# Prompt attention on one core: outputs one unit later in TensorE's order, with second buffers for the transposed weights

## The reference

```python
s_c = einsum(q, kc) * scale + bias ; p_c = masked_softmax(s_c) ; o_c = p_c @ vc
s_s = einsum(q, k_sel) * scale + bias ; p_s = masked_softmax(s_s) ; o_s = p_s @ v_sel
s_w = einsum(q, kw) * scale + bias ; p_w = masked_softmax(s_w) ; o_w = p_w @ vw
o = g[..., 0:1] * o_c + g[..., 1:2] * o_s + g[..., 2:3] * o_w
```

## Time and profile before

| | |
|---|---|
| median of three runs | 1896.12 us |
| profiled execution | 1892.59 us |
| its span | 1890.8 us |
| mean granted clock of TensorE | 0.954 |
| TensorE matmul busy | 1770.0 us, 94% |
| VectorE busy | 836.6 us, 44% |
| ScalarE busy | 525.2 us, 28% |
| prompt attention, first scores to last weighted sum | 201.7 to 329.2 us |

### The profile page before, as it was taken

How to read it: one execution, slowest core, us unless ns; L and a number is a source line. 1 busy time by engine, 2 the same in 40 slices (tenths; PEclk the granted TensorE clock), 3 DMA queues, 4 the chain that set the end, 5 groups by cost and what they waited for, 6 DMA issues and landing times. The chain is left out here.

```text
span 1890.8 us, 36210 instructions
## 1 busy us (share of the span) xinstructions
PE 1770.0 (94%) x15772; PEld 1690.7 (89%) x15772; DVE 836.6 (44%) x1654; ACT 525.2 (28%) x896; POOL 696.1 (37%) x278
## 2 busy tenths in 40 slices
PE   6989798779768999899999999999999999999997
PEld 6987688569745998799999999999999999999997
DVE  4251586225573444465430355444235555024531
ACT  5132454322241222232221222331223222112221
POOL 1300000012202111355653555655655655445641
PEclk8988699989978999899999999999999999999999
DMA  5540420513200100122222222322222222222222
GB/s 146 122 57 23 148 90 13 162 48 94 60 1 22 37 4 28 46 89 90 68 73 85 88 90 65 92 91 90 68 89 90 68 90 73 84 90 90 66 78 76
DMA packets 158379, 140.90 MB, mean 75 GB/s; under 512 B 16178, under 2 KB 153942, under 8 KB 157838
## 3 DMA queue, kind: packets, MB, share of 16 engines
q1 hardware_dynamic: 158222, 138.60, 24.8%
HBM read 132.68 MB, written 10.02 MB: 75 GB/s over the span
## 5 line engine op out<-in xcount | busy, mean ns | idle before, releaser
L270 POOL TENSOR_TENSOR w_lo<-w_raw,w_hi 128x2048 fp32r<-128x2048 f32 (+3 forms) x109 | 459.3, 4214 | 783.9 <-ACT w_hi L264 783.7
L309 PE MATMUL ps<-h_hi,w_hi 128*128 128x288 f32 x2016 | 434.1, 296 | 0.0
L309 PE MATMUL ps<-h_hi,w_lo 128*128 128x288 f32 x2016 | 433.4, 296 | 0.0
L309 PE MATMUL ps<-h_lo,w_hi 128*128 128x288 f32 x2016 | 433.2, 296 | 0.0
L264 ACT ACTIVATE w_hi<-w_raw 128x2048 fp32r<-128x2048 f32 (+3 forms) x109 | 190.1, 1744 | 501.9 <-PE ps L309 458.5
L309 PEld LDWEIGHTS ps<-h_hi,w_hi 128*128 128x128 f32 x2016 | 324.0, 189 | 0.3
L309 PEld LDWEIGHTS ps<-h_hi,w_lo 128*128 128x128 f32 x2016 | 323.7, 189 | 0.0
L309 PEld LDWEIGHTS ps<-h_lo,w_hi 128*128 128x128 f32 x2016 | 323.5, 189 | 0.0
L418 DVE TENSOR_TENSOR xT<-ps,xT 128x576 f32<-128x576 f32 x48 | 35.6, 756 | 264.7 <-PE ps L309 264.7
L309 PE MATMUL ps<-g_lo,w_hi 128*128 128x288 f32 x704 | 151.1, 295 | 0.0
L309 PE MATMUL ps<-g_hi,w_lo 128*128 128x288 f32 x704 | 151.0, 295 | 0.0
(11 more groups left out here) (497 smaller groups left out, 2794.5 us busy)
## 6 DMA issues: line engine op xcount, KB each, us to landing
w_raw<-in_ffn_up SPq DMA_DIRECT2D x44, 1024.0 KB, 5.0
w_raw<-in_ffn_down SPq DMA_DIRECT2D x16, 768.0 KB, 4.8
w_raw<-in_w_in_odd SPq DMA_DIRECT2D x12, 1024.0 KB, 5.1
w_raw<-in_ffn_down SPq DMA_DIRECT2D x16, 640.0 KB, 4.4
w_raw<-in_w_in_even SPq DMA_DIRECT2D x7, 1024.0 KB, 5.4
w_raw<-in_w_in_even SPq DMA_DIRECT2D x6, 872.0 KB, 9.6
BT<-rv SPq DMA_DIRECT2D x8, 520.0 KB, 3.6
seg<-in_cache_cmp_kv SPq DMA_DIRECT2D x32, 128.0 KB
```

The lines of the kernel that those rows point to most:

```text
L270: pool.tensor_tensor(slab_view(wlo[slot], st), slab_view(raw[slot], st), slab_view(whi[slot], st).bitcast(F32), ALU.subtract).then_inc(w_l ...
L309: last = pe.matmul(ps[:, bank + 2 * j + half, 0:HT], w[slot][:, c:c + 128], x[:, xs + t, half * HT:(half + 1) * HT], start=(t == 0 and n = ...
```

## The change

TensorE's order in the loop becomes: transposes of unit u, outputs of unit u-1, scores of unit u+2; the outputs of the last unit follow behind the loop. On VectorE the weighted sum of unit u-1 moves ahead of `masked_max(u+2)`, behind the copy of PTw and the factors of unit u. The buffers PTs, PTw and PTc are doubled, and den has four rows in place of two; ScalarE and VectorE wait for the outputs of two units back before they write the copies, and `exps(u)` waits for the weighted sum of unit u-4 and not u-2. The wait for `s_taken` ahead of the small transpose stays as it is, and so do all shapes, the number of instructions on the data, and the DMAs.

```diff
@@ tensor
+                    def outputs(u):
+                        h, qt, s = u // 4, u % 4, u % 2
+                        g = h // 4
+                        pe.wait_ge(pt_act, u + 1)
+                        pe.wait_ge(pt_dve, u + 1)
+                        if u >= 1:
+                            pe.wait_ge(o_taken, u)
+                        O = ps[:, 7, 0:192]
+                        pe.matmul(O[:, 0:64], PTc[s][:, :], vc[0:32, 2, 64 * g:64 * g + 64], start=True, stop=True)
+                        for n, (PT, c0) in enumerate(((PTs[s], 896), (PTw[s], 1152))):
+                            for kt in range(qt + 1):
+                                last = pe.matmul(O[:, 64 * (n + 1):64 * (n + 2)], PT[:, kt, :], zq[:, kt, c0 + 64 * g:c0 + 64 * g + 64],
+                                                 start=(kt == 0), stop=(kt == qt))
+                        last.then_inc(o_ready, 1)
...
                         pe.transpose(ps[0:32, 4, 256:384], sC[s][:, :], ident[:, :]).then_inc(pt_ready, 1)
+                        if u >= 1:
+                            outputs(u - 1)
                         if u + 2 < U:
                             scores(u + 2)
-                        pe.wait_ge(pt_act, u + 1)
-                        pe.wait_ge(pt_dve, u + 1)
-                        if u >= 1:
-                            pe.wait_ge(o_taken, u)
...
+                    outputs(U - 1)
@@ vector
                         dve.wait_ge(pt_ready, u + 1)
+                        if u >= 2:
+                            dve.wait_ge(o_ready, u - 1)
+                        dve.tensor_copy(PTw[s][:, 0:qt + 1, :], ps[:, 6, 0:128 * (qt + 1)].rearrange("p (a b) -> p a b", b=128)).then_inc(pt_dve, 1)
...
                         if u >= 1:
+                            weighted(u - 1)
                         if u + 2 < U:
                             masked_max(u + 2)
+                    weighted(U - 1)
@@ scalar
-                        if u >= 2:
-                            act.wait_ge(o_taken, u - 1)
+                        if u >= 4:
+                            act.wait_ge(o_taken, u - 3)
...
-                        if u >= 1:
-                            act.wait_ge(o_ready, u)
+                        if u >= 2:
+                            act.wait_ge(o_ready, u - 1)
```

More of the change, by code:

```diff
@@ L1508, in even_mixer @@
             sC = [r.take("s_cmp", [128, 32]) for _ in range(2)]
-            PTs = r.take("PTs", [128, 4, 128])
-            PTw = r.take("PTw", [128, 4, 128])
-            PTc = r.take("PTc", [32, 128])
+            PTs = [r.take("PTs", [128, 4, 128]) for _ in range(2)]
+            PTw = [r.take("PTw", [128, 4, 128]) for _ in range(2)]
+            PTc = [r.take("PTc", [32, 128]) for _ in range(2)]
             mx = r.take("mx", [128, 2, 3])
-            den = r.take("den", [128, 2, 3])
+            den = r.take("den", [128, 4, 3])
             bt_in, s_ready, s_taken, p_ready, pt_ready, pt_act, pt_dve, o_ready, o_taken, m_ready = (sem(x) for x in (
@@ L1572, in _ @@
                         h, qt, s = u // 4, u % 4, u % 2
-                        g = h // 4
                         pe.wait_ge(p_ready, u + 1)
@@ L1620, in masked_max, with weighted @@
                         dve.tensor_scalar(mx[:, s, :], mx[:, s, :], -1.0, None, ALU.mult).then_inc(m_ready, 1)
+                    def weighted(u):
+                        h, qt, s = u // 4, u % 4, u % 2
+                        dve.wait_ge(o_ready, u + 1)
+                        O, out = ps[:, 7, 0:192], onat[:, qt, 64 * h:64 * h + 64]
+                        dve_chain(dve, dve.tensor_scalar(out, O[:, 0:64], den[:, u % 4, 0:1], None, ALU.mult))
+                        dve_chain(dve, dve.scalar_tensor_tensor(out, O[:, 64:128], den[:, u % 4, 1:2], out, ALU.mult, ALU.add))
+                        dve.scalar_tensor_tensor(out, O[:, 128:192], den[:, u % 4, 2:3], out, ALU.mult, ALU.add).then_inc(o_taken, 1)
                     masked_max(0)
@@ L1625, in _ @@
                         dve.wait_ge(pt_ready, u + 1)
-                        if u >= 1:
[L1627 to L1633, removed]
+                        if u >= 2:
+                            dve.wait_ge(o_ready, u - 1)
+                        dve.tensor_copy(PTw[s][:, 0:qt + 1, :], ps[:, 6, 0:128 * (qt + 1)].rearrange("p (a b) -> p a b", b=128)).then_inc(pt_dve, 1)
+                        dve.wait_ge(p_ready, u + 1)
+                        dve_chain(dve, dve.tensor_scalar(den[:, u % 4, :], den[:, u % 4, :], 1e-30, None, ALU.max))
+                        dve_chain(dve, dve.reciprocal(den[:, u % 4, :], den[:, u % 4, :]))
+                        dve_chain(dve, dve.tensor_tensor(den[:, u % 4, :], den[:, u % 4, :], gpr[:, qt, 3 * h:3 * h + 3], ALU.mult))
+                        if u >= 1:
+                            weighted(u - 1)
                         if u + 2 < U:
                             masked_max(u + 2)
[L1636 to L1640, removed]
+                    weighted(U - 1)
                 @block.scalar
@@ L1647, in exps @@
                         act.wait_ge(m_ready, u + 1)
-                        if u >= 2:
-                            act.wait_ge(o_taken, u - 1)
-                        act.activation(sC[s][:, :], sC[s][:, :], ACT.Exp, bias=mx[:, s, 0:1], accum_out=den[:, s, 0:1])
-                        act.activation(sS[s][:, 0:nk], sS[s][:, 0:nk], ACT.Exp, bias=mx[:, s, 1:2], accum_out=den[:, s, 1:2])
-                        act.activation(sW[s][:, 0:nk], sW[s][:, 0:nk], ACT.Exp, bias=mx[:, s, 2:3], accum_out=den[:, s, 2:3]).then_inc(p_ready, 1)
+                        if u >= 4:
+                            act.wait_ge(o_taken, u - 3)
+                        d = u % 4
+                        act.activation(sC[s][:, :], sC[s][:, :], ACT.Exp, bias=mx[:, s, 0:1], accum_out=den[:, d, 0:1])
+                        act.activation(sS[s][:, 0:nk], sS[s][:, 0:nk], ACT.Exp, bias=mx[:, s, 1:2], accum_out=den[:, d, 1:2])
+                        act.activation(sW[s][:, 0:nk], sW[s][:, 0:nk], ACT.Exp, bias=mx[:, s, 2:3], accum_out=den[:, d, 2:3]).then_inc(p_ready, 1)
                     exps(0)
                     for u in range(U):
-                        qt = u % 4
+                        qt, s = u % 4, u % 2
                         act.wait_ge(pt_ready, u + 1)
-                        if u >= 1:
-                            act.wait_ge(o_ready, u)
-                        act.copy(PTc[:, :], ps[0:32, 4, 256:384]).then_inc(ptc_act, 1)
-                        act.copy(PTs[:, 0:qt + 1, :], ps[:, 5, 0:128 * (qt + 1)].rearrange("p (a b) -> p a b", b=128)).then_inc(pt_act, 1)
+                        if u >= 2:
+                            act.wait_ge(o_ready, u - 1)
+                        act.copy(PTc[s][:, :], ps[0:32, 4, 256:384]).then_inc(ptc_act, 1)
+                        act.copy(PTs[s][:, 0:qt + 1, :], ps[:, 5, 0:128 * (qt + 1)].rearrange("p (a b) -> p a b", b=128)).then_inc(pt_act, 1)
                         if u + 1 < U:
```

## The result

The changed kernel takes 1959.82 us (median of 4 runs, 1945.9 to 1971.02) where the kernel before takes 1894.51: a ratio of 1.0336, 95% interval 1.0297 to 1.0374, slower by some 64 us. Forecast were slower, +16.5 us and a range up to 1932. The direction and the wait behind it were right; the time was out of the range, because rival (a), to which the forecast gave 15%, came true in nearly the whole stage; the sign that the forecast gave for it, a mean granted clock under 0.9 between 232 and 312 us, reads 0.56. In this study the interval of a ratio is about 0.2 to 0.5% wide to each side. One execution of e3_buffers, 2223 us at a mean clock of 0.73 where the others have 0.95, is left out of its ratio.

A forecast was written before the change was run, and what follows sets the result against it. TensorE, busy 1770.0 of 1890.8 us, was taken as the bound, with the uncovered maxima lengthening its beat: 13.0 + 1.7 + 0.4 - 0.7 - 0.9 + 3.0 = +16.5 us, so 1912.6 us. Range 1903 to 1924, widened to 1902 and 1932.

The forecast's parts named there:

- rival (a): Prompt attention: TensorE's clock falls or doesn't rise for several heads, 8 to 10 us each; four heads +36 us; 15%.
- The wait: Small transpose of the next unit waits for masked_max(u+2), uncovered in the new order: 15 to 25 us instead of 0.3.
- The new beat: Steps between small transposes in prompt attention: 4.64, 3.79, 3.73, 3.86 us, 16.02 a head against 13.85, +2.2 us a head.
- The end: Last small transpose to last weighted sum: 5.4 us at full clock, 9.1 at the low, against 5.65; +3.0 us taken.
- The clock: Prompt attention: TensorE idles at most 0.9 us at a time, under the 1.15 us before an earlier fall; clock stays up.
- the first rival: The same as rival (a): the clock falls, or doesn't rise, for several heads; 1948 us; 15%.
- The buffers: Second buffers and four denominator rows: 0 in the forecast, at most 1.8 us of gain from the exponentials' waits.
- Rival (b): Faster: masked_max(u+2) is done in time and TensorE's slots set the beat, 12.4 us a head; -10 us, 1886; 5%.
- Rival (c): Within 0.5%: half the uncovered maxima hidden by TensorE's queue, 1.2 us a head less; +8 us, 1904; 13%.

The follow-up runs named there:

- e3_buffers: The kernel before with only the change's doubled buffers, four denominator rows and their waits, order untouched; ratio 1.0013 to the kernel before.
- e1_bank: The changed kernel with the small transpose in another PSUM bank, so it no longer waits for masked_max(u+2); ratio 1.0014 to the kernel before, 1899.9 us.
- e4_order: The changed kernel with outputs of u-1 behind scores of u+2, and the weighted sum behind masked_max; ratio 0.9976 to the kernel before.
- e2_filler: The changed kernel with six more transposes ahead of the wait for the maxima in units of q = 0, 1, 2; ratio 1.0062 to the kernel before.
- e6_gap_long: The kernel before with the small transpose waiting for a GpSimd addition of 250 to 550 columns; ratio 1.0238 to the kernel before, 1934.21 us.
- e7_fill2: The changed kernel with two more transposes ahead of the wait in units of q = 0, 1, 2; ratio 1.019 to the kernel before, 1929.89 us.
- e11_warm_only: The changed kernel with 14 identity transposes during the wait for the first bias table; ratio 1.0279 to the kernel before, 1945.94 us.
- e9_stores: Outputs of u-1 behind scores of u+2, and stores of keys and values moved behind head 2's bias table; ratio 0.9996 to the kernel before, 1894.4 us.
- e8_warm: Outputs of u-1 behind scores of u+2, plus identity transposes where TensorE waits at the stage's start and end; ratio 1.002 to the kernel before, 1895.31 us.
- e10_best: Outputs behind scores, stores moved behind head 2's table, identity transposes at the stage's start and end; ratio 0.9973 to the kernel before, 1890.08 us.

## Why the prediction was wrong, point by point

**The wait** was right. The prediction named the place (the small transpose of the next unit behind masked_max), the loop and its row; the trace after has 24 waits there, and e1_bank and e4_order, which remove it in two ways, both win back the whole 64 us. Two details were off. The 15 to 25 us forecast are met by the weight loads (17.2), not by the matmuls (6.7) whose 0.3 us they were set against; and the longest wait at the high clock stands after a step from q = 3 (0.95 us), not from q = 0. The earlier trace rows show only that the program's semaphore holds TensorE there: no run drops the wait and stays in bank 4, so that it must stay there was not tested.

**The new beat** was right where its condition held: 16.02 us a head forecast, 16.3 in e2_filler, and the two steps of the changed kernel at the high clock within 0.2 us. e2_filler comes out at +12 and not +16.5, since its clock rose earlier and was still up at the end: its units 0 to 3 took 14.81 us (210.93 to 225.74), 5.8 less than in the changed kernel, and its end 6.33, which takes 4.7 and 2.3 us off the forecast terms; the six heads add 1.9.

**The end** was right: 9.1 us at the low clock forecast, 9.27 measured.

**The step that failed** is the one under "The clock": "No gap is as long as the one of the earlier trace rows; I take it that the clock stays up." One gap of 1.15 us with a fall behind it was read as the least that makes the clock fall. The trace gave no ground for this: it had two short waits a head, of 0.3 and 0.4 us, and no stretch with a gap in nearly every unit, which is what the change made. Gaps of 0.3 to 1.0 us that come back in most units held the clock low for most of the stage, and e6_gap_long shows it apart from the order; e2_filler and e7_fill2, which fill the gaps and keep the order, and e11_warm_only, where a raised clock falls again, agree. The page "TensorE: Matmul & The Clock Gate" of the Trainium skill ("A second HAM failure mode: psum-queue depth-cycling") was weighed there and put aside; by that rule the first rival would have been the forecast, and the measurement agrees with it.

**The size of rival (a).** Its price, 8 to 10 us a head, is borne out: 24.82 - 16.28 = 8.5. It was multiplied by four heads. Of the 27 steps from unit 4 on, 21 are at the low clock, 2 are mixed and 4 at the high one, so about five and a half heads: 16.5 + 47 = +63, against +64 measured. So one term, the number of heads at the low clock, was mis-sized, and the range, whose upper end took in only a part of this rival, was too narrow by that.

**The buffers** were costed at 0, and e3_buffers has 1.0013 +- 0.0025. **Rival (b)**, faster, fell with the first row of the waits. **Rival (c)** fell with e2_filler, where nothing of the maxima is hidden by TensorE's queue.

Still open: why the clock rises some 24 us behind the first scores in the kernel before, but 14 us behind them in e1_bank and 7 in e2_filler, and why it dips once in e4_order (260 to 263 us) and e9_stores without a gap in the trace. Part of this differs between executions of one kernel: the kernel before took 1881.98 us at a mean clock of 0.962 and 1906.95 at 0.949.

## What to carry to other kernels

When a wait is moved, ask what the waiting engine does between the producer's start and the wait: here the old order hid masked_max under the outputs, and swapping two groups of TensorE took that cover away, while the delay of the outputs by a unit was useful all along (e4_order). Price an idle time on TensorE twice, as itself and at the low clock, and let the range reach to the low clock for the whole stage if the gap comes back in every iteration. And after an engine becomes faster, read the waits for DMAs again: twice a table that had been early enough was late, and only with both groups of transfers moved behind the tables did the gain of 13 us appear.

## What the runs showed of the hardware

Useless work can pay: 144 transposes more made the changed kernel 53 us faster (1959.82 to 1907.08), as they kept the granted clock at 1.00 from 216 to 328 us. Idle times of 0.36 to 0.72 us in most units, put into an otherwise unchanged kernel, cost 45 us in 32 units (1.0238 of 1892), about twice what they cost at the high clock (at most 21 us) or could come to by themselves (32 times 0.72 is 23 us). And a single idle time of TensorE of 2.9 us (e8_warm) or 2.3 us (e10_best) behind a late table was followed by 12 to 24 us at the low clock, at steps of 5 to 7 us where they are 3 to 4.
